# First token tile of an encoder layer loaded in two column halves, its squares split half, quarter, quarter, and one preset moved

## The chip, the cores and the metric

One core of one Trainium2 chip. The metric is device time of one execution in microseconds (us); three runs of the kernel before are given. Everything on the core is written out by hand: five engines (TensorE = PE, VectorE = DVE, ScalarE = ACT, GpSimd = POOL, SyncE = SP) each run their own list of instructions in order and wait for each other by semaphores.

## The reference

One layer of an encoder over 512 tokens of width 1024, in float32. The part that matters here is its head:

```python
u = rmsnorm(h, g_pre_mix[i])        # y = x * rsqrt(mean(x*x) + 1e-6) * g
proj = u @ w_in[i]                  # 1024 x 3840
qa, ka, va, qb, kb, vb, qc, kc, vc = jnp.split(proj, SPLIT_POINTS, axis=-1)
```

Behind it come three kinds of attention, gates, an output product with a norm and a residual, and a feed-forward part with a convolution of width 3, again with norms and a residual.

## The kernel before

The 512 tokens are four tiles of 128 (`x_tok[:, t, :]`, t = 0 to 3, token on the partition). Matrix products are made from float32 values split in a high and a low part: `high*high + high*low + low*high`, three matmuls each. So each operand needs a rounded copy (ACT, `w_hi`, `u_high`) and a difference (POOL `w_lo` for weights, DVE `u_low` for tokens).

The head of the program, tile by tile:

- SP issues the loads of tiles 0 and 1 (`load_x`, L636), then the first two weight tiles (L670, L654, L655), tiles 2 and 3, two more weight tiles, and the small tables (`load_small`, L642 to L650). Weight tiles go into a ring of four places.
- ACT squares and sums tiles 1 and 3 whole and tile 0's first 512 columns (`square`, L1046), into `norm_ss`. DVE sums the squares of tile 0's other 512 columns (L1605), already divided by 1024 and with the epsilon added, into `norm_ms`, and of tile 2 whole (L1622).
- POOL's `rstd` makes the mean (L882) and the power -0.5 (L885). For tile 0 it waits for both sums, by `squares` and `first_square`. Between these it makes the low quarters of the first weight tiles (`w_lo_quarter`, L899; later ones in `w_lo`, L871): its order is mean and power of tiles 0 and 1, four quarters of weight tile 0, one of weight tile 1, mean and power of tile 2, three quarters, mean and power of tile 3.
- DVE scales each tile by its power and the gain (tile 0 in two halves, L1611; the others L1591). The gain has been spread over the partitions by two matmuls (L2356).
- PE transposes the scaled tiles (L2362 for tile 0, L2342 for the others) and multiplies with the first two weight tiles (`value_products`, L2508) in an order written out by hand: tile 0 high by high, transposes of tile 1, tile 0 the rest, tile 1, transposes of tile 2, and so on. A few transposes of the identity (`keep_clock_up`, L2350) fill its time before.
- Before tile 0 is there, DVE presets four pieces of memory (L1600 to L1603). The last of them, `pages[0:CHUNK, Q_LO_PG:Q_LO_PG + 2, :]`, 64 x 1024 zeros, is needed by the first score product (`pe.wait_ge(q_lo_cleared, 2)` ahead of `qk(0)`).

## Time and profile before

| | |
|---|---|
| median of 3 runs | 841.32 us (840.88, 841.32, 843.56) |
| profiled execution, its own time | 841.03 us |
| its span, first to last instruction | 839.2 us |
| TensorE busy | 831.0 us (99%) |
| VectorE, ScalarE, GpSimd busy | 647.0, 478.9, 398.6 us |
| granted TensorE clock, mean | 0.999 |

The profile is of one execution. Its page gives busy time by engine, the chain of work that ended last, and groups of instructions; the trace can be asked for the timeline of a stretch, the waits, and the traffic. Times in rows are us from the start of the span, so they compare with 839.2, and the 1.8 us between span and time stand outside.

### The profile page before, as it was taken

To read this page: it belongs to the slowest core of one execution; us is meant where nothing else is said; L and a number is where in the kernel's file an instruction comes from. 1 tells how busy PE (TensorE), PEld (TensorE's weight loads), DVE (VectorE), ACT (ScalarE), POOL (GpSimd) and SP (SyncE) were. 2 spreads that over 40 slices of the span, in tenths; PEclk is the share of its full clock that TensorE was granted. 3 is DMA by queue.
4 is the path that set the end of the run, shared out by engine and by line. 5 is a ranking of instruction groups with operands and counts; after the bars stand their busy time and mean duration, and the time that the engine had idled before them with its cause. 6 is when DMAs were issued, how large, how long until landed. Compare 5 with 4: busy or idle time off the path is not lost.

```text
span 839.2 us, 13423 instructions
## 1 busy us (share of the span) xinstructions
PE 831.0 (99%) x4701; PEld 727.0 (87%) x4701; DVE 647.0 (77%) x1263; ACT 478.9 (57%) x905; POOL 398.6 (47%) x511
## 2 busy tenths in 40 slices
PE   8999999999999999999999999999999999999997
PEld 7888888888888888999998899899999999988885
DVE  6577777788776867966544389988888888999995
ACT  5475656777776664544443447556565656545662
POOL 6454434433352346986677426766565656010002
PEclk9999999999999999999999999999999999999999
DMA  7632133232223212334336631555554443396584
GB/s 238 175 102 73 53 100 100 75 99 57 82 80 69 80 44 82 114 114 120 95 101 218 201 134 52 187 174 170 170 171 118 121 119 121 132 312 242 170 285 157
DMA packets 138071, 111.35 MB, mean 133 GB/s; under 512 B 7607, under 2 KB 121215, under 8 KB 136724
## 3 DMA queue, kind: packets, MB, share of 16 engines
q1 hardware_dynamic: 136378, 102.05, 40.0%
q0 software_dynamic: 720, 5.24, 1.8%
q10 hardware_dynamic: 906, 3.20, 1.1%
q8 instruction: 38, 0.62, 0.3%
q14 instruction: 29, 0.24, 0.1%
HBM read 97.05 MB, written 13.42 MB: 132 GB/s over the span
## 4 chain that ended last, share of the span: by engine, by line
PE 97%; DVE 1%; DMA 0%; ACT 0%; issue 0%; POOL 0%; DVEq 0%; POOLq 0%
PE banks L2324 24%; PE banks L2326 24%; PE banks L2325 24%; PE banks L2626 3%; PE banks L2625 3%; PE banks L2624 3%; PE banks L2498 2%; PE banks L2407 2%; PE banks L2406 2%; PE banks L2794 1%; PE banks L2793 1%; PE banks L2795 1%; PE banks L2508 1%; PE banks L2470 1%; PE banks L2477 1%; PE banks L2342 1%
## 5 line engine op out<-in xcount | busy, mean ns | idle before, releaser
L871 POOL TENSOR_TENSOR ring_lo<-ring_raw,ring_hi 128x256 fp32r<-128x256 f32 x376 | 305.5, 846 | 278.1 <-ACT ring_hi L1036 277.8
L2324 PE MATMUL banks<-u_hi,ring_hi 128*128 128x512 f32 (+1 forms) x580 | 222.0, 383 | 0.0
L2326 PE MATMUL banks<-u_hi,ring_lo 128*128 128x512 f32 (+1 forms) x580 | 217.4, 375 | 0.0
L2325 PE MATMUL banks<-u_lo,ring_hi 128*128 128x512 f32 (+1 forms) x580 | 217.1, 374 | 0.0
L2326 PEld LDWEIGHTS banks<-u_hi,ring_lo 128*128 128x128 f32 x580 | 109.2, 188 | 20.0
L2325 PEld LDWEIGHTS banks<-u_lo,ring_hi 128*128 128x128 f32 x580 | 109.5, 189 | 18.1
L2324 PEld LDWEIGHTS banks<-u_hi,ring_hi 128*128 128x128 f32 x580 | 109.3, 188 | 17.8
L1036 ACT CAST ring_hi<-ring_raw 128x1024 fp32r<-128x1024 f32 x95 | 99.0, 1043 | 38.7 <-PE banks L2326 22.9
L2145 DVE SCALAR_TENSOR_TENSOR wide<-banks,cols,wide 128x511 f32<-128x511 f32 x88 | 64.6, 744 | 3.5 <-ACT wide L1402 1.6
L2324 PE MATMUL banks<-pages,ring_hi 128*128 128x512 f32 (+1 forms) x180 | 61.2, 340 | 0.0
L2325 PE MATMUL banks<-pages,ring_hi 128*128 128x512 f32 (+1 forms) x180 | 61.2, 340 | 0.0
L2326 PE MATMUL banks<-pages,ring_lo 128*128 128x512 f32 (+1 forms) x180 | 61.1, 340 | 0.0
L1191 ACT ACTIVATE scratch<-scratch,negmax 128x193 f32<-128x193 f32 (+5 forms) x96 | 49.4, 517 | 8.4 <-DVE negmax L1796 7.6
L882 POOL TENSOR_SCALAR norm_ms<-norm_ss 128x1 f32<-128x1 f32 x14 | 4.4, 311 | 95.2 <-ACT pages L1046 94.9
L1796 DVE CUSTOM_DVE_ANT_0 scratch<-banks,scratch 128x128 f32<-128x128 f32 (+3 forms) x64 | 28.9, 488 | 24.4 <-PE banks L2498 23.2
L2324 PE MATMUL banks<-ring_hi,pages 128*128 128x512 f32 x112 | 44.0, 393 | 0.0
L2326 PE MATMUL banks<-ring_hi,pages 128*128 128x512 f32 x112 | 43.6, 389 | 0.0
L2325 PE MATMUL banks<-ring_lo,pages 128*128 128x512 f32 x112 | 43.6, 389 | 0.0
L962 POOL TENSOR_TENSOR ring_lo<-ring_raw,ring_hi 128x256 fp32r<-128x256 f32 x44 | 37.6, 874 | 11.7 <-ACT ring_hi L1430 11.7
L1402 ACT ACTIVATE wide<-banks,cols 128x512 f32<-128x512 f32 x40 | 31.1, 776 | 21.1 <-DVE banks L2119 13.4
L2326 PEld LDWEIGHTS banks<-pages,ring_lo 128*128 128x128 f32 x180 | 34.2, 190 | 3.8
L2324 PEld LDWEIGHTS banks<-pages,ring_hi 128*128 128x128 f32 x180 | 34.2, 190 | 3.5
(339 smaller groups left out, 2004.7 us busy)
## 6 DMA issues: line engine op xcount, KB each, us to landing
ring_raw<-in_w_ffn_up_dram SPq DMA_DIRECT2D x88, 256.0 KB, 3.5
ring_raw<-in_w_in_dram SPq DMA_DIRECT2D x59, 256.0 KB, 3.4
ring_raw<-in_w_ffn_down_dram SPq DMA_DIRECT2D x55, 256.0 KB, 3.7
ring_raw<-in_w_gate_dram SPq DMA_DIRECT2D x48, 256.0 KB, 3.3
split_tokens<-pages SPq DMA_DIRECT2D x5, 1024.0 KB, 7.0
pages<-split_tokens POOLq DMA_DIRECT2D x5, 1024.0 KB, 6.6
ring_raw<-in_w_out_dram SPq DMA_DIRECT2D x16, 256.0 KB, 3.1
second_tokens<-wide SPq DMA_DIRECT2D x10, 384.0 KB, 3.9
```

Source lines behind the costliest of these rows:

```text
L871: last = pool.tensor_tensor(wlo[:, r, c], raw[:, r, c], whi[:, r, c].bitcast(F32), ALU.subtract)
L962: last = pool.tensor_tensor(dst[:, c], src[:, c], hi[:, c].bitcast(F32), ALU.subtract)
L1036: act.copy(whi[:, r, :], raw[:, r, :]).then_inc(w_hi_done, 1)
L1191: act.activation(p_out, p_in, ACT.Exp, scale=-1.0, bias=negmax[:, s % 2, m:m + 1], accum_out=rowsum[:, s % 2, m:m + 1]).then_inc(exp_done, 1)
L1402: act.activation(wide[:, 4 + 2 * j + c, :], psum[:, 2 * j + c, :], ACT.Identity, scale=cols[:, 88 + fc:89 + fc], bias=cols[:, 132 + fc:133 ...
L1796: dve.tensor_tensor_reduce(scratch[:, P_PAGE + m, c0:c0 + n], psum[:, SC_BANK + m, 0:n], scratch[:, BIAS_PAGE + b % 4, j0:j0 + n], -1.0, c ...
L2145: dve.scalar_tensor_tensor(out=y[:, back:SEQ], in0=psum[:, 2 * j + c, 0:SEQ - back], scalar=tap, in1=y[:, back:SEQ], op0=ALU.mult, op1=ALU ...
L2324: pe.matmul(out, lhs_hi, rhs_hi, start=start, stop=False)
L2325: pe.matmul(out, lhs_hi, rhs_lo, start=False, stop=False)
L2326: return pe.matmul(out, lhs_lo, rhs_hi, start=False, stop=stop)
L2624: pe.matmul(dst, w_h, u_h, start=False, stop=False, skip_group_check=True)
L2625: pe.matmul(dst, w_h, u_l, start=False, stop=False, skip_group_check=True)
```

## The change

Tile 0 is loaded by two DMAs, columns 0 to 511 with a semaphore of its own, `x_first`, and columns 512 to 1023 with `x_loaded[0]`. DVE sums the squares of the first half as soon as that is there, and then those of columns 768 to 1023, starting from the first sum; ACT squares columns 512 to 767 only. POOL waits for two counts of `first_square`. The second preset of q moves from ahead of the sums to between the scaling of tiles 2 and 3. The small loads use one semaphore fewer among them.

```diff
-        small_loaded = [sem(f"small_loaded{i}") for i in range(5)]
+        small_loaded = [sem(f"small_loaded{i}") for i in range(4)]
+        x_first = sem("x_first")
...
-            load_x(0)
+            sp.dma_start(x_tok[:, 0, 0:512], x_rows[0][:, 0:512]).then_inc(x_first, 16)
+            sp.dma_start(x_tok[:, 0, 512:1024], x_rows[0][:, 512:1024]).then_inc(x_loaded[0], 16)
             load_x(1)
...
-                    sp.dma_start(lam_in[:, i, :], v[0].partition_broadcast(P)).then_inc(small_loaded[4], 16)
-                sp.dma_start(sink[:], sinks[0].partition_broadcast(P)).then_inc(small_loaded[1], 16)
+                    sp.dma_start(lam_in[:, i, :], v[0].partition_broadcast(P)).then_inc(small_loaded[1], 16)
+                sp.dma_start(sink[:], sinks[0].partition_broadcast(P)).then_inc(small_loaded[0], 16)
...
-                    pool.wait_ge(first_square, 1)
+                    pool.wait_ge(first_square, 2)
...
-            square(0, 0, x_tok[:, 0, 0:512], 512)
+            square(0, 0, x_tok[:, 0, 512:768], 256)
...
-            dve.memset(pages[0:CHUNK, Q_LO_PG:Q_LO_PG + 2, :].bitcast(F32), 0.0).then_inc(q_lo_cleared, 1)
+            dve.wait_ge(x_first, 16)
+            dve.tensor_tensor_reduce(tmp[:, 0:512], x_tok[:, 0, 0:512], x_tok[:, 0, 0:512], 1.0 / D, EPS,
+                                     ALU.mult, ALU.add, norm_ms[:, 0, 3:4]).then_inc(first_square, 1)
             dve.wait_ge(x_loaded[0], 16)
-            dve.tensor_tensor_reduce(tmp[:, 0:512], x_tok[:, 0, 512:1024], x_tok[:, 0, 512:1024], 1.0 / D, EPS,
-                                     ALU.mult, ALU.add, norm_ms[:, 0, 0:1]).then_inc(first_square, 1)
+            dve.wait_ge(first_square, 1)
+            dve.tensor_tensor_reduce(tmp[:, 512:768], x_tok[:, 0, 768:1024], x_tok[:, 0, 768:1024], 1.0 / D,
+                                     norm_ms[:, 0, 3:4], ALU.mult, ALU.add, norm_ms[:, 0, 0:1]).then_inc(first_square, 1)
...
-            dve.wait_ge(first_square, 1)
+            dve.wait_ge(first_square, 2)
...
-            for t in (2, 3):
-                xs(0, t, x_tok[:, t, :], spread_gain())
+            xs(0, 2, x_tok[:, 2, :], spread_gain())
+            dve.memset(pages[0:CHUNK, Q_LO_PG:Q_LO_PG + 2, :].bitcast(F32), 0.0).then_inc(q_lo_cleared, 1)
+            xs(0, 3, x_tok[:, 3, :], spread_gain())
...
-                dve.wait_ge(small_loaded[4], 64)
+                dve.wait_ge(small_loaded[1], 64)
...
-                dve.wait_ge(small_loaded[0], 16)
+                dve.wait_ge(small_loaded[0], 2 * 16)
...
-                dve.wait_ge(small_loaded[1], 16)
```

The head of VectorE's list before (`ISA` is the sum of squares, with the read of its accumulator behind it):

```order
L1603 MEMSET pages 64x1024
L1605 ISA wide,norm_ms<-scratch 128x512 [waits x_loaded0]
L1605 ISA norm_ms 128x1
L1611 SCALAR_TENSOR_TENSOR scratch<-scratch,norm_rstd,banks 128x512 [waits gain_spread,rstd_done]
...
L1597 TENSOR_TENSOR u_lo<-banks,u_hi 128x8x128 [waits u_hi_done]
L1591 SCALAR_TENSOR_TENSOR scratch<-scratch,norm_rstd,banks 128x1024 [waits rstd_done] x2
```

and now, with the line numbers of the changed program:

```order
L1606 ISA wide,norm_ms<-scratch 128x512 [waits x_first]
L1606 ISA norm_ms 128x1
L1610 ISA wide,norm_ms<-scratch,norm_ms 128x256 [waits first_square,x_loaded0]
L1610 ISA norm_ms 128x1
L1616 SCALAR_TENSOR_TENSOR scratch<-scratch,norm_rstd,banks 128x512 [waits gain_spread,rstd_done]
...
L1599 TENSOR_TENSOR u_lo<-banks,u_hi 128x8x128 [waits u_hi_done]
L1593 SCALAR_TENSOR_TENSOR scratch<-scratch,norm_rstd,banks 128x1024 [waits rstd_done]
L1631 MEMSET pages 64x1024
L1593 SCALAR_TENSOR_TENSOR scratch<-scratch,norm_rstd,banks 128x1024 [waits rstd_done]
```

One sum of squares has become two, of which the second waits for the first, and the preset has moved behind the scaling of tile 2.

The head of SyncE's list before:

```order
L636 DMA scratch<-in_x_dram 128x1024 x2
L670 DMA ring_raw<-in_w_in_dram 128x2x256
```

and now:

```order
L639 DMA scratch<-in_x_dram 128x512
L640 DMA scratch<-in_x_dram 128x512
L637 DMA scratch<-in_x_dram 128x1024
L672 DMA ring_raw<-in_w_in_dram 128x2x256
```

Tile 0 takes two places in the queue, and everything behind it stands one place later.

## Rows read from the trace of the kernel before

**Rows 1.** The page, part 4: chain that ended last, by engine.
```profile
PE 97%; DVE 1%; DMA 0%; ACT 0%; issue 0%; POOL 0%; DVEq 0%; POOLq 0%
```
**Rows 2.** Waits of PE, whole span (us in total, times, longest us).
```profile
PE banks L2362 <- DVE scratch L1611: 0.5, 1, 0.5
PE banks L2508 <- ACT u_hi L1050: 0.2, 1, 0.2
```
**Rows 3.** Chain of waits in order of time, start (start us, us, what).
```profile
0.74 4.03 DMA scratch<-in_x_dram
...
5.72 0.28 POOL norm_ms L882
...
6.07 0.56 POOL norm_rstd L885
...
6.66 0.76 DVE scratch L1611
7.42 0.04 issue
...
8.88 0.94 PE banks L2508 x4
```
**Rows 4.** Timeline, first 15 us (start us, us, engine, instructions, [idle before]).
```profile
0.74 0.87 SPq L636 DMA_DIRECT2D scratch<-in_x_dram  x2
...
3.53 0.91 DVE L1603 MEMSET pages<- 64x1024 f32 x1 [0.27 <-issue]
...
4.79 0.63 ACT L1046 ACTIVATE pages<-scratch 128x512 fp32r<-128x512 f32 x1 [2.20 <-DMA scratch<-in_x_dram]
4.80 0.69 DVE L1605 CUSTOM_DVE_ANT_0 wide<-scratch 128x512 f32<-128x512 f32 x1 [0.36 <-DMA scratch<-in_x_dram]
...
6.08 1.06 ACT L1046 ACTIVATE pages<-scratch 128x1024 fp32r<-128x1024 f32 x1 [0.57 <-DMA scratch<-in_x_dram]
...
7.60 0.55 POOL L885 TENSOR_TENSOR norm_rstd<-norm_ms,minus_half 128x1 f32<-128x1 f32 x1
...
8.19 1.28 DVE L1591 SCALAR_TENSOR_TENSOR scratch<-scratch,norm_rstd,banks 128x1024 f32<-128x1024 f32 x1
...
9.66 1.03 PE L2342 MATMUL banks<-ident,scratch 128*128 128x128 f32 x8
...
13.58 1.28 DVE L1591 SCALAR_TENSOR_TENSOR scratch<-scratch,norm_rstd,banks 128x1024 f32<-128x1024 f32 x1 [0.40 <-POOL norm_rstd L885]
...
14.91 1.09 PE L2342 MATMUL banks<-ident,scratch 128*128 128x128 f32 x8
```
**Rows 5.** Traffic by stretch (last number GB/s); tile 2's issue and landing.
```profile
3.75:4.00 0.25, 0.25 (x3) 0.25 (x2) 0.25 (x1) 0.00 (x0) 0.00 (x0) 1.00 0.97 393
...
7.00:7.50 0.50, 0.04 (x1) 0.04 (x1) 0.50 (x2) 0.50 (x3) 0.17 (x1) 1.00 0.92 318
...
4.82 0.94 SPq L636 DMA_DIRECT2D scratch<-in_x_dram  x2
...
scratch<-in_x_dram SPq DMA_DIRECT2D x1, 512.0 KB, 5.8
```
**Rows 6.** Timeline of POOL's weight quarters and of VectorE, 8 to 17 us.
```profile
8.13 1.43 POOL L899 TENSOR_TENSOR ring_lo<-ring_raw,ring_hi 128x256 fp32r<-128x256 f32 x2
...
10.91 1.73 POOL L899 TENSOR_TENSOR ring_lo<-ring_raw,ring_hi 128x256 fp32r<-128x256 f32 x1
...
10.66 1.37 DVE L1622 CUSTOM_DVE_ANT_0 wide<-scratch 128x1024 f32<-128x1024 f32 x1
...
11.96 1.21 DVE L1597 TENSOR_TENSOR u_lo<-banks,u_hi 128x1024 fp32r<-128x1024 f32 x1
...
13.41 1.12 PE L2508 MATMUL banks<-ring_hi,u_lo 128*128 128x256 f32 x8
...
16.59 1.28 DVE L1591 SCALAR_TENSOR_TENSOR scratch<-scratch,norm_rstd,banks 128x1024 f32<-128x1024 f32 x1 [1.73 <-POOL norm_rstd L885]
```
**Rows 7.** Stretch of PE's first products (granted clock third from the end).
```profile
8.50:9.00 0.50, 0.39 (x4) 0.18 (x3) 0.50 (x1) 0.50 (x2) 0.50 (x2) 1.00 0.83 315
```

## The prediction

> **What bounds the kernel now.** I read the page first, then the waits of TensorE, then the chain of waits at the start, then the timeline of the first 20 us. The page's chain lies for 97% on TensorE [rows 1]. After its first instruction TensorE waits only twice in the whole execution: 0.5 us for the scaled token tile 0 and 0.2 us for the high part of tile 2 [rows 2]. So this is a kernel in which a delay or a gain before 20 us reaches the end one to one, and nothing later gives it back; and the change touches only what happens before 17 us. The question is what the start waits for.
>
> The chain at the start [rows 3] goes: landing of token tile 0 (0.74 + 4.03 = 4.77), ScalarE's squares, POOL's mean at 5.72 and power at 6.07, VectorE's scaling at 6.66, TensorE's transposes, first products at 8.88. The reader should see that this chain is drawn by the last releaser alone, and that a second chain runs beside it: tile 1. ScalarE idles 0.57 us and starts tile 1's squares at 6.08, on the landing; POOL's power for tile 1 ends at 7.60 + 0.55 = 8.15; VectorE, free about 0.1 us before, scales tile 1 from 8.19 to 9.47; TensorE transposes it from 9.66 [rows 4]. From POOL's 8.15 on hang also the low weight quarters, after them the mean of tile 2, its scaling 13.58 to 14.86, and its transposes on TensorE at 14.91 [rows 4]. VectorE's end at 7.42 (6.66 + 0.76) is taken up by TensorE at 7.46, so 0.04 us suffice between the two engines [rows 3]. Tile 1's chain is therefore only 0.19 - 0.04 = 0.15 us behind at 9.66 and 0.05 - 0.04 = 0.01 us behind at 14.91. **Tile 0 is not the only thing that the start waits for.**
>
> **The change, part by part.**
> 1. The load of tile 0 in two halves. SyncE issues two DMAs of 512 KB in 0.87 us [rows 4], so one more costs 0.43 us of its queue. The first half lands earlier than 4.77: 262 kB at the 393 GB/s that flowed from 3.75 to 4.00 [rows 5] are 0.67 us, so at about 4.10. The second half ends with the same last byte, at 4.77. Tile 1's issue moves from about 1.18 to 1.6, but its bytes flow only after tile 0's (tile 0 lands at 4.77, tile 1 at 6.08, 1.3 us for 524 kB, which is the full rate), so the later issue is covered by the backlog; if it were not, it would cost its 0.43. The same holds for tile 2, issued at 4.82 and landed 5.8 us later [rows 5]. Rows of 2 KB in place of 4 KB: the nearest rows are 393 GB/s where 4 KB rows flow and 318 GB/s in a stretch with 1 KB rows of weights [rows 5]; if all of tile 0 went at the lower rate it would take 1.65 instead of 1.33 us, +0.3. I take +0.03, as 2 KB is nearer to the large rows and most of the low rate is in mixed traffic. Bounds of this part for tile 1: 0 and +0.43.
> 2. Squares. ScalarE's 512 columns took 0.63 and 1024 took 1.06 [rows 4], so 256 take 0.63 - 0.21 = 0.42: 0.21 less. VectorE's 512 columns took 0.69 [rows 4]; 256 take 0.35 to 0.42. The first half's sum starts at 4.10 and ends with its accumulator read near 4.9, about 0.1 after the second half is there, because the second instruction waits for the first. It ends at about 5.3, ScalarE's at about 5.3 too. So POOL's mean starts at about 5.55 instead of 5.72: **-0.17** on tile 0's chain. Bounds: -0.21 if the first half lands by 3.95, and +0.4 if it lands no sooner than the whole (0.69 and then another 0.35 to 0.42, in a row).
> 3. The second preset of q leaves the place before the sums. Its 0.91 us from 3.53 to 4.44 [rows 4] were free, since the tile landed at 4.77; left there it would have held up the new first sum by 0.3. Now it stands between the scaling of tiles 2 and 3, where VectorE idled 1.73 us before 16.59 waiting for POOL [rows 6]: 14.86 + 0.91 = 15.77, done 0.8 before that. Cost 0 for VectorE; its reader, the first score product, is at the 39th microsecond. What is behind that cover is POOL: in that gap it does the last low quarter of weight tile 1 and the mean and power of tile 3. Nearest row for VectorE holding up POOL: a quarter takes 0.7 (two in 1.43), but the one from 10.91 took 1.73, beside the sum over tile 2 on VectorE from 10.66 to 12.04 [rows 6]. If the preset did the same, tile 3's scaling at 16.59 would slip by up to 0.91. So 0 to +0.91; I take 0, because the nearest row's instruction reads two operands from SBUF and a preset reads none.
>    The Trainium skill says the same in "SBUF — State Buffer", section on which engines share a port: a VectorE instruction with two SBUF inputs contends with a reading GpSimd instruction, one with at most one input outside the two-port modes does not. By that page the 1.73 us quarter is the lock, on which the trace agrees, and the sum has 0 for the preset; by the 1.73 us row alone it would be +0.9.
> 4. Semaphores of the small loads merged. The readers at 23 and 27 us come well after those landings; the extra SyncE issue may shift them by 0.43. Cost 0.
>
> **Sum.** Tile 0's chain gains 0.17. At 9.66 TensorE can use 0.15 of it, at 14.91 only 0.01 to 0.05, since tile 2's transposes hang on tile 1's landing by way of POOL. Tile 1 pays 0.03. Net: -0.05 + 0.03, or about -0.02. From the profiled execution's own 841.03 that is 841.0; the median of the three runs lies 0.29 above it, so **841.3** on that scale. What a measurement of this kernel can tell from no change is 0.3%, 2.5 us; I forecast that nothing can be told.
>
> **The rivals.**
> *The whole gain of tile 0 arrives.* For it: the chain of waits names tile 0 alone. Against it: the 0.01 us of room at 14.91. It would need tile 1 to land earlier too. Then -0.17 to -0.67 (the full head start of the first half): 840.6 to 841.1. Chance 0.12.
> *The lock changes its order.* VectorE's sum over tile 2 started at 10.66, inside POOL's fourth quarter, and got the port when that ended at 10.91 [rows 6]. Tile 2 is issued at 4.82 and lands 5.8 us later, at 10.62: only 0.04 before VectorE asks. If it lands more than 0.25 us later (one more DMA issue is 0.43), POOL's fifth quarter goes first, the sum starts at 11.6 and the low part of tile 1 behind it, which ended at 11.96 + 1.21 = 13.17, ends 0.7 to 0.8 late; TensorE took it up at 13.41 [rows 6] and so had about 0.2 us of room: +0.5, or 841.8. With the upper bound for tile 1's own landing added, +0.9, 842.2. Speaking against it is the backlog. Chance 0.11, slower but under 2.5 us. The Trainium skill, "DMA: Bandwidth & Descriptors", rules for kernel authors, speaks against splitting: many small transfers should be coalesced into one, and two transfers to disjoint partition halves serialize, since both use all 16 engines; column halves as here do so too. By that the first half buys little and tile 1 pays; the sum would be this rival's. No row here shows a split load.
> *The preset holds up POOL*, as in part 3: +0.9, 842.2. Chance 0.06.
> *TensorE runs slower for a stretch.* This one alone could be told from no change. The four products from 8.88 took 0.94 us, some 0.22 each from start to start [rows 3], while eight of the same shape took 1.12 from 13.41, 0.12 each [rows 6]; the granted clock reads 1.00, the 2.4 GHz level, in the stretch around 8.88 [rows 7], so the record doesn't settle what slows them. With the change TensorE has products done at about 9.4 and idles up to 0.2 us before 9.66, where it was busy. If the slow pace lasted on from there, each product would cost 0.1 more; some 25 of them make the 2.5 us, that is if the slow pace held until about 13 us. Against it: the idle before 7.46 gets shorter, not longer. 843.8 or more, chance 0.03.
>
> **How the numbers follow.** The forecast has 0.68, the rivals 0.12, 0.11, 0.06 and 0.03. Only the last leaves the 0.3%. From the forecast's share I give 0.01 to slower and 0.02 to faster by over 2.5, for what I haven't seen and for the scatter: one of three runs stood at 843.56, 2.2 above the median. Faster 0.02, within 0.94, slower 0.04. Range: the lowest run, 840.88, less the 0.17 and a little, is 840.6, with the tail of the first rival 840.5; upward the second and third rivals end at 842.2. So 840.5 to 842.2, leaving out the scatter and the clock.
>
> **What would show it.** Right: the first sum on VectorE starts about 4.1, POOL's first mean at 5.55, first transposes of tile 0 at about 7.3; ScalarE's squares of tile 1 still start near 6.08, tile 1's transposes near 9.6, tile 2's within 0.1 of 14.9; the quarter of 1.7 us is still there; VectorE's preset near 14.9 with quarters of 0.7 beside it; span 839.1 to 839.3. Wrong: squares of tile 1 before 5.9 or after 6.3; a POOL quarter beside the preset over 1 us; tile 2's transposes moved by over 0.2 either way; slow products past 9.7; or a TensorE wait after 20 us that wasn't there.

## The result and the profile after

| | before | changed | |
|---|---|---|---|
| median of 14 runs each, same chip | 840.93 us | 842.38 us | ratio 1.0018, 95% interval 1.001 to 1.0026 |
| lowest run | 840.37 | 841.25 | +0.88 |
| profiled execution | 841.03 | 842.04 | +1.01 |
| its span | 839.2 | 840.2 | +1.0 |

The change costs about 1 us in a single execution and 1.45 us between the medians (1.8 parts in a thousand, 0.8 to 2.2 us by the interval). That is within the 0.3% called "no change", but it isn't zero. The median lies above the range, which ended at 842.2; the profiled execution, 842.04, lies inside it. The runs scatter upward: 6 of the changed kernel's 14 took 843.8 us or more, where 2 of the 14 before took 843.6, so the shift of the medians is less sure than the 1.0 us of the two traces.

The page's chain is as before, 97% TensorE:

```profile
PE 97%; DVE 1%; DMA 1%; ACT 0%; issue 0%; DVEq 0%; SPq 0%; POOL 0%
```

The waits of TensorE over the whole span of the changed kernel (us in total, times, longest us), beside [rows 2]:

```profile
PE banks L2513 <- ACT u_hi L1063: 1.2, 1, 1.2
PE banks L2347 <- DVE scratch L1593: 0.2, 1, 0.2
PE banks L2513 <- ACT u_hi L1052: 0.2, 1, 0.2
```

The wait of 0.5 us for the scaled tile 0 [rows 2] is gone. There are two new ones: 0.2 for the scaled tile 1 (VectorE, L1593), and 1.2 ahead of tile 0's own first products, which stand before tile 1's transposes. They need ScalarE's rounded copy of tile 0 (`u_hi`, L1063). TensorE was ready for them early, since tile 0 came early. But ScalarE works through its list in order, and there the squares of tile 1 stand ahead of that copy. So tile 1's late landing holds up tile 0 as well: its first products start at 9.43, 0.55 later than before (8.88 [rows 3]), though its mean came earlier. This adds nothing to the loss, as TensorE then waits 0.2 for tile 1 all the same. The chain of waits at the start leads back to tile 1 (start us, us, what):

```profile
0.74 0.40 SPq L639
...
1.19 0.42 SPq L640
...
1.66 5.45 DMA scratch<-in_x_dram
...
7.14 1.16 ACT pages L1048 x2
...
8.38 0.20 POOL norm_ms L884
...
8.66 0.56 POOL norm_rstd L887
...
9.24 1.29 DVE scratch L1593
...
10.58 1.09 PE banks L2347 x8
```

In [rows 3] this chain began with tile 0's landing at 4.77. Now it begins with three issues on SyncE's queue, and the long piece is the landing of tile 1, issued at 1.66 and there at 7.11. The timeline of the first 27 us shows both tiles (start us, us, engine, instruction, [idle before <- releaser]):

```profile
1.66 0.52 SPq L637 DMA_DIRECT2D scratch<-in_x_dram  x1
...
3.62 0.69 DVE L1606 CUSTOM_DVE_ANT_0 wide<-scratch 128x512 f32<-128x512 f32 x1 [0.35 <-DMA scratch<-in_x_dram]
...
4.21 0.42 ACT L1048 ACTIVATE pages<-scratch 128x256 fp32r<-128x256 f32 x1 [1.62 <-DMA scratch<-in_x_dram]
...
4.47 0.49 DVE L1610 CUSTOM_DVE_ANT_0 wide<-scratch,norm_ms 128x256 f32<-128x256 f32 x1 [0.15 <-DVE norm_ms L1606]
...
5.18 0.26 POOL L884 TENSOR_SCALAR norm_ms<-norm_ss,norm_ms 128x1 f32<-128x1 f32 x1 [3.71 <-DVE norm_ms L1610]
...
7.14 1.06 ACT L1048 ACTIVATE pages<-scratch 128x1024 fp32r<-128x1024 f32 x1 [2.42 <-DMA scratch<-in_x_dram]
...
8.71 0.58 ACT L1063 CAST u_hi<-banks 128x512 fp32r<-128x512 f32 x1
...
9.43 0.93 PE L2513 MATMUL banks<-ring_hi,u_hi 128*128 128x256 f32 x4 [1.19 <-ACT u_hi L1063]
...
15.95 1.09 PE L2347 MATMUL banks<-ident,scratch 128*128 128x128 f32 x8
...
26.20 0.40 PE L2329 MATMUL banks<-u_hi,ring_hi 128*128 128x512 f32 x1
```

The reader should see three things. The first half was there by 3.6 and the second by 4.2, where the whole tile had landed at 4.77; POOL's mean came 0.54 earlier (5.18 against 5.72 [rows 3]). Tile 1's squares start 1.06 later (7.14 against 6.08 [rows 4]). And from there the delay is handed on undiminished: tile 1's transposes 10.58 against 9.66, tile 2's 15.95 against 14.91 [rows 4], and the first product of full width 26.20 against 25.17 in the kernel before.

The traffic of the changed kernel in five stretches of one microsecond (last number GB/s, ahead of it the busy share of the DMA engines):

```profile
1.50:2.50 1.00, 0.97 (x5) 0.97 (x6) 0.73 (x3) 1.00 (x1) 0.00 (x0) 1.00 0.53 170
2.50:3.50 1.00, 1.00 (x6) 1.00 (x5) 0.76 (x1) 0.09 (x1) 0.00 (x0) 1.00 0.96 344
3.50:4.50 1.00, 1.00 (x5) 0.77 (x4) 0.73 (x3) 0.29 (x1) 0.00 (x0) 1.00 0.82 289
4.50:5.50 1.00, 1.00 (x2) 0.34 (x1) 0.46 (x2) 0.22 (x2) 0.26 (x1) 1.00 0.85 284
5.50:6.50 1.00, 1.00 (x4) 0.36 (x3) 0.38 (x1) 0.00 (x0) 0.56 (x1) 1.00 0.67 206
```

and the same stretches of the kernel before:

```profile
1.50:2.50 1.00, 0.97 (x5) 0.97 (x6) 0.73 (x3) 1.00 (x1) 0.00 (x0) 1.00 0.62 115
2.50:3.50 1.00, 1.00 (x6) 1.00 (x5) 0.76 (x1) 0.09 (x1) 0.00 (x0) 1.00 0.92 258
3.50:4.50 1.00, 1.00 (x4) 0.77 (x4) 0.91 (x1) 0.00 (x0) 0.00 (x0) 1.00 1.02 401
4.50:5.50 1.00, 1.00 (x2) 0.34 (x1) 0.70 (x2) 0.71 (x2) 0.00 (x0) 1.00 0.98 375
5.50:6.50 1.00, 1.00 (x4) 0.44 (x3) 0.00 (x0) 0.43 (x2) 0.70 (x2) 1.00 1.08 377
```

A rate in GB/s over one microsecond is a number of kB, so the sums are what had moved by 6.5: 170 + 344 + 289 + 284 + 206 = 1293 kB after, 1526 before. The changed kernel is ahead until 3.5 us (514 against 373) and then moves 374 kB less in the next three microseconds, at 206 to 289 GB/s. The engines were busy for 0.82, 0.85 and 0.67 of these, against 1.02, 0.98 and 1.08 before. They weren't short of work: by 4.63 SyncE had issued tiles 0 and 1 and two weight tiles, 2.1 MB. A stretch between 3.5 and 6.5 us in which the busy share is under 0.9 is called a hole below.

Which rows moved can be read from the sizes of the packets. From 4.5 us on a row of tile 1 is a packet of 4 KB (in the kernel before the first few may still be tile 0's), a row of weights one of 1 KB, and those under 512 B carry no rows of either. The changed kernel, 4.5 to 5.5 and 5.5 to 6.5:

```profile
DMA packets 186, 0.28 MB, mean 284 GB/s; under 512 B 14, under 2 KB 151, under 8 KB 186
DMA packets 147, 0.21 MB, mean 206 GB/s; under 512 B 15, under 2 KB 124, under 8 KB 147
```

and the kernel before, in the same two stretches:

```profile
DMA packets 177, 0.37 MB, mean 375 GB/s; under 512 B 15, under 2 KB 109, under 8 KB 177
DMA packets 403, 0.38 MB, mean 377 GB/s; under 512 B 35, under 2 KB 403, under 8 KB 403
```

Before, 94 rows of weights and 68 of tokens start in the first stretch, and none of tile 1's in the second: tile 1 is through, and then come the weights. In the changed kernel 137 rows of weights and 35 of tile 1 start in the first, 109 and 23 in the second. So tile 1's last rows trail behind while weights that were issued after it already move, and the engines stand idle for a third of the second stretch. This view doesn't tell the 16 engines apart, so it doesn't say which of them trail.

The preset, at its new place, on VectorE:

```profile
16.05 0.91 DVE L1631 MEMSET pages<- 64x1024 f32 x1 [0.15 <-issue]
```

and POOL's low quarter of a weight tile beside it:

```profile
15.95 0.72 POOL L901 TENSOR_TENSOR ring_lo<-ring_raw,ring_hi 128x256 fp32r<-128x256 f32 x1
```

The quarter takes half of what two took in [rows 6], 1.43 / 2. The preset doesn't hold it up.

### The profile page after: what moved, and what is told of

It reads as the page before. It is cut to its first block, busy times and chain, and to the rows that moved or that the text cites. A ratio compares the mean times of both kernels' runs of the same rounds, so it can differ in the third digit from the quotient of the medians.

```text
span 840.2 us, 13427 instructions
## 1 busy us (share of the span) xinstructions
PE 831.3 (99%) x4701; PEld 727.0 (87%) x4701; DVE 648.9 (77%) x1265; ACT 478.4 (57%) x905; POOL 398.4 (47%) x511
## 4 chain that ended last, share of the span: by engine, by line
PE 97%; DVE 1%; DMA 1%; ACT 0%; issue 0%; DVEq 0%; SPq 0%; POOL 0%
PE banks L2329 24%; PE banks L2331 24%; PE banks L2330 24%; PE banks L2631 3%; PE banks L2629 3%; PE banks L2630 3%; PE banks L2503 2%; PE banks L2412 2%; PE banks L2411 2%; PE banks L2800 1%; PE banks L2798 1%; PE banks L2799 1%; PE banks L2513 1%; PE banks L2475 1%; PE banks L2482 1%; PE banks L2347 1%
```

## The experiments

All runs are set against the kernel before on the same chip in the same job. One table serves them all. "Tile 1" is the start of ScalarE's squares of tile 1; where ScalarE was still busy with tile 0, the landing was no later, which the table marks with ≤. "Full product" is the start of TensorE's first product of width 512 (25.17 before). "Rest" is the span less that start. kB is what had moved by 6.5 us. The ratio is worked out from the single runs and isn't the quotient of the two medians.

| kernel | place of tile 1's load | tile 1 | full product | span | rest | kB | median / before | ratio, 95% interval |
|---|---|---|---|---|---|---|---|---|
| before | SyncE, 2nd | 6.08 | 25.17 | 839.2 | 814.0 | 1526 | | |
| changed | SyncE, 3rd | 7.14 | 26.20 | 840.2 | 814.0 | 1293 | 842.38 / 840.93 | 1.0018, 1.001 to 1.0026 |
| e1 | SyncE, 2nd | 5.85 | 25.82 | 839.8 | 814.0 | 1560 | 841.58 / 841.17 | 1.0004, 0.9994 to 1.0014 |
| e2 | SyncE, 3rd | 7.55 | 26.60 | 840.6 | 814.0 | 1287 | 842.84 / 841.17 | 1.0015, 1.0 to 1.0029 |
| e3 | SyncE, 2nd | 5.86 | 25.30 | 839.4 | 814.1 | 1555 | 841.28 / 841.17 | 0.9997, 0.9985 to 1.0009 |
| e4 | SyncE, 2nd | 5.89 | 25.33 | 839.4 | 814.1 | 1607 | 841.67 / 841.17 | 1.0003, 0.9991 to 1.0015 |
| e5 | SyncE, 3rd | 6.38 | 25.84 | 839.8 | 814.0 | 1421 | 842.3 / 841.28 | 1.0014, 1.0002 to 1.0026 |
| e6 | ScalarE | ≤5.86 | 25.42 | 839.5 | 814.1 | 1591 | 841.35 / 841.28 | 1.0007, 0.9996 to 1.0019 |
| e7 | SyncE, 3rd and 4th | 6.88 | 25.95 | 840.0 | 814.1 | 1309 | 841.94 / 841.28 | 1.0007, 0.9997 to 1.0016 |
| e8 | SyncE, 3rd | 8.29 | 27.35 | 842.6 | 815.3 | 922 | 844.54 / 841.28 | 1.0036, 1.0022 to 1.0051 |
| e9 | SyncE, 2nd, issued later | 5.63 | 25.85 | 843.0 | 817.2 | 1476 | 842.0 / 841.12 | 1.0009, 0.9997 to 1.0021 |
| e10 | SyncE, 2nd | ≤6.40 | 25.93 | 839.9 | 814.0 | 1484 | 842.38 / 841.12 | 1.0017, 1.0005 to 1.0029 |
| e11 | SyncE, 5th | 6.88 | 25.92 | 839.9 | 814.0 | 1278 | 842.34 / 841.12 | 1.0015, 1.0005 to 1.0024 |
| e12 | SyncE, 3rd | 7.23 | 26.29 | 840.2 | 813.9 | 1266 | 842.0 / 841.12 | 1.0004, 0.9994 to 1.0013 |
| e13 | SyncE, 3rd | 7.55 | 26.62 | 840.7 | 814.1 | 1431 | 844.12 / 841.18 | 1.0045, 1.0026 to 1.0063 |
| e14 | ScalarE | 6.64 | 25.70 | 839.8 | 814.1 | 1602 | 841.87 / 841.18 | 1.0011, 1.0001 to 1.0021 |
| e15 | SyncE, 2nd | 5.96 | 25.02 | 839.1 | 814.1 | 1609 | 841.16 / 841.18 | 1.0004, 0.9994 to 1.0013 |

Read the column "rest" first. In 15 of 17 executions it is 813.9 to 814.1, whatever the start did; the full products start anywhere between 25.02 and 26.62. So **the span is 814.0 plus the start of the full product**, and an experiment on the start can be read from its trace to 0.1 us where the medians scatter by several tenths. The two exceptions, e8 and e9, have late waits of their own. The waits of TensorE in e9:

```profile
PE banks L2794 <- ACT banks L1570: 1.2, 1, 1.2
PE banks L2325 <- DVE u_lo L2215: 0.9, 1, 0.9
PE banks L2509 <- DVE u_lo L1598: 0.5, 1, 0.5
```

The first two end at 768 and 793 us; e8 has one of 0.9 us, ending at 793. In the other 15 profiled executions they don't occur, and [rows 2] don't show them.

### Which part of the change costs: e1, e2, e3, e12

**e1_whole_load**: the changed kernel, tile 0 loaded by one DMA.

```diff
-        x_first = sem("x_first")
...
-            sp.dma_start(x_tok[:, 0, 0:512], x_rows[0][:, 0:512]).then_inc(x_first, 16)
-            sp.dma_start(x_tok[:, 0, 512:1024], x_rows[0][:, 512:1024]).then_inc(x_loaded[0], 16)
+            load_x(0)
...
-            dve.wait_ge(x_first, 16)
+            dve.wait_ge(x_loaded[0], 16)
```

> Changed kernel with tile 0 loaded whole again; the squares stay split half, quarter, quarter. If the split load is the cause: squares of tile 1 at about 6.1 us; tile 0's mean on POOL starts later than before the change, about 6.1 instead of 5.72, since the sums over 512 and 256 columns run in a row after 4.77; tile 1's transposes at 9.7 to 10.0; time 0 to 0.4 us above before. If the squares or the preset are the cause, it stays 1 to 1.5 us above.

Tile 1 is back at 5.85. But without the half load VectorE's two sums stand in a row, POOL's mean comes at 6.15 instead of 5.72, and the full product at 25.82. The time, 0.4 us over before, is that of the squares' split without its early half, no longer that of tile 1.

**e2_split_load_only**: the kernel before, tile 0 by two DMAs, all else as it was.

```diff
-            load_x(0)
+            for h in range(2):
+                c = slice(512 * h, 512 * (h + 1))
+                sp.dma_start(x_tok[:, 0, c], x_rows[0][:, c]).then_inc(x_loaded[0], 16)
             load_x(1)
...
-            act.wait_ge(x_loaded[0], 16)
+            act.wait_ge(x_loaded[0], 32)
```

(The same wait on VectorE.)

> Kernel before with tile 0 loaded by two DMAs from SyncE, all else as before (both readers wait for both halves). If the split load itself makes tile 1 late: ScalarE's squares of tile 1 start near 7.1 us instead of 6.08, tile 1's transposes near 10.6 instead of 9.66, and the time is 1 to 1.5 us above the kernel before. If the split load is harmless and the new order of squares or the preset is to blame: squares of tile 1 at 6.1, time within 0.3 us of before.

The timeline of ScalarE in e2:

```profile
7.55 1.06 ACT L1048 ACTIVATE pages<-scratch 128x1024 fp32r<-128x1024 f32 x1 [2.48 <-DMA scratch<-in_x_dram]
```

This one edit brings tile 1's late landing, the wait for ScalarE's copy of tile 0 (here 1.5 us), and a full product at 26.60. It is the whole loss, and more.

**e3_preset_only**: the kernel before, with only the preset moved.

```diff
-            dve.memset(pages[0:CHUNK, Q_LO_PG:Q_LO_PG + 2, :].bitcast(F32), 0.0).then_inc(q_lo_cleared, 1)
...
-            for t in (2, 3):
-                xs(0, t, x_tok[:, t, :], spread_gain())
+            xs(0, 2, x_tok[:, 2, :], spread_gain())
+            dve.memset(pages[0:CHUNK, Q_LO_PG:Q_LO_PG + 2, :].bitcast(F32), 0.0).then_inc(q_lo_cleared, 1)
+            xs(0, 3, x_tok[:, 3, :], spread_gain())
```

> Kernel before with the second preset of q moved between the scaling of tiles 2 and 3. If the preset does not hold up POOL: the POOL quarter beside it takes 0.7 us, tile 3 is scaled from 16.6 us, time within 0.3 us of before. If it holds the port: a quarter of 1 us or more, tile 3 scaled up to 0.9 us later, time up to 0.9 us above.

No difference (ratio 0.9997). VectorE in e3 from 10.6 us on:

```profile
10.68 1.81 DVE L1621 CUSTOM_DVE_ANT_0 wide<-scratch 128x1024 f32<-128x1024 f32 x1 [0.24 <-DMA scratch<-in_x_dram]
...
14.98 0.91 DVE L1625 MEMSET pages<- 64x1024 f32 x1 [0.16 <-issue]
```

and POOL:

```profile
9.28 2.13 POOL L899 TENSOR_TENSOR ring_lo<-ring_raw,ring_hi 128x256 fp32r<-128x256 f32 x3
...
13.38 2.13 POOL L899 TENSOR_TENSOR ring_lo<-ring_raw,ring_hi 128x256 fp32r<-128x256 f32 x3
```

The three quarters from 13.38 take 0.71 each, and the preset at 14.98 lies across the third: again not held up. VectorE's line at 10.68 is the prediction's second rival, come by chance of the landing: tile 2 was a little late, VectorE's sum started 0.01 us after POOL's fifth quarter (10.67), and it took 1.81 us instead of 1.37 [rows 6]. The price was a wait of 0.3 us on TensorE (for the low part of tile 1), where 0.5 was said. The same order is in e1, e5 and e9, with waits of 0.2, 0.4 and 0.5 us.

**e12_changed_again**: the changed kernel once more, unedited.

> The changed kernel as it is, profiled a second time. If tile 1's late landing belongs to the change: squares of tile 1 again at 7 or later and 1 to 1.5 us above before. If it was an accident of one execution: squares near 6.1 to 6.5.

The trace repeats: tile 1 at 7.23, full product 26.29, span 840.2. The medians differ by less here (842.0 against 841.12) than in the first comparison (842.38 against 840.93). Where the trace says 1.0, two comparisons of medians said 1.45 and 0.9, and the interval of the second, 0.9994 to 1.0013, by itself doesn't exclude that nothing changed.

### Why tile 1 lands late: e4, e5, e6, e7, e9, e10, e11, e8

**e4_half_from_act**: the second half is issued on ScalarE's queue (at 0.75 us), so tile 1 is again second on SyncE's.

```diff
-            sp.dma_start(x_tok[:, 0, 512:1024], x_rows[0][:, 512:1024]).then_inc(x_loaded[0], 16)
...
+            act.dma_start(x_tok[:, 0, 512:1024], x_rows[0][:, 512:1024]).then_inc(x_loaded[0], 16)
             act.dma_start(g_row, g_pre_mix).then_inc(small_loaded[2], 16)
```

> Changed kernel with the second half of tile 0 issued on ScalarE's queue, ahead of the gain row, so that tile 1 has the second place in SyncE's queue again (issue near 1.2 us). If the later place in SyncE's queue is what makes tile 1 late: it lands near 6.1, squares of tile 1 at 6.1, time at or 0.1 to 0.3 us below before. If it is the two loads of 2 KB rows as such: squares of tile 1 stay near 7.1 and the time 1 to 1.5 us above before.

Tile 1 is there at 5.89. The rows are 2 KB as in the changed kernel, so rows of 2 KB alone don't delay it (though only one load of such rows is left ahead of it on its queue). But now the halves land together (the first sum on VectorE starts at 4.50), and POOL's mean comes at 6.07.

**e6_tile1_from_act**: the changed kernel, with tile 1 on ScalarE's queue behind the gain row.

```diff
-            load_x(1)
...
             act.dma_start(g_row, g_pre_mix).then_inc(small_loaded[2], 16)
+            act.dma_start(x_tok[:, 1, :], x_rows[1]).then_inc(x_loaded[1], 16)
```

> Changed kernel with tile 1 issued on ScalarE's queue behind the gain row, near 1.3 us, and both halves of tile 0 on SyncE's. If tile 1's late issue or its third place in SyncE's queue is the cause: squares of tile 1 at about 6.1, tile 0's mean on POOL still near 5.2, time 0 to 0.3 us below before. If not: squares of tile 1 above 7, time 1 us or more above before.

Traffic in e6:

```profile
1.50:2.50 1.00, 0.96 (x5) 0.97 (x6) 0.73 (x3) 0.81 (x1) 0.00 (x0) 1.00 0.58 131
2.50:3.50 1.00, 1.00 (x6) 1.00 (x5) 0.76 (x1) 0.47 (x1) 0.00 (x0) 1.00 0.94 326
3.50:4.50 1.00, 1.00 (x5) 0.78 (x4) 0.70 (x2) 0.00 (x0) 0.00 (x0) 1.00 1.01 387
4.50:5.50 1.00, 1.00 (x2) 0.34 (x1) 0.05 (x1) 0.05 (x1) 0.00 (x0) 1.00 0.98 367
5.50:6.50 1.00, 1.00 (x3) 0.34 (x1) 0.44 (x2) 1.00 (x3) 0.27 (x1) 1.00 1.09 380
```

The hole is gone, and tile 1 is there by 5.86. But it now shares the engines with tile 0's second half, which lands at 5.45; POOL's mean comes at 6.16, where 5.2 was expected. What tile 1 got back, tile 0 paid. The issue is only 0.36 us earlier than in the changed kernel (1.30 against 1.66), the landing at least 1.25. In the Trainium skill, "DMA: Bandwidth & Descriptors", section "Issuing engines are not separate DMA queues", a second issuing engine saves only the time of issue. Here that page and the measurement differ: on a second queue the load gained over three times what its issue gained. And with tile 0 whole the same move made it later (e14).

**e5_weights_held**: the changed kernel, SyncE waits for the first half before it issues weights (first weight DMA at 3.52).

```diff
+            sp.wait_ge(x_first, 16)
             for t, (kind, n) in enumerate(TILES):
```

> Changed kernel in which SyncE waits for the first half of tile 0 (landed at 3.6 us) before it issues the first weights. If weights issued from 2.2 us on slow tile 1's rows: tile 1 lands at 5.9 to 6.1, its squares start 1 us sooner than in the changed kernel, and the weights come later by up to 1.4 us. If tile 1 is late for its own place or rows: squares of tile 1 still at 7.1 or later.

Tile 1 at 6.38, between the two expectations: some 0.8 of the 1.06 is back, so in the changed kernel weights issued after tile 1 take engine time that tile 1 needs, as the packets above show too. Everything behind is issued later as well, tile 2 at 5.91 instead of 4.67. VectorE's sum of tile 2 starts only at 11.75, TensorE waits 0.4 us for the low part of tile 1, and the full product is at 25.84.

**e7_both_tiles_split**: tile 1 too is loaded in two column halves, third and fourth on the queue.

```diff
-            load_x(1)
+            for h in range(2):
+                c = slice(512 * h, 512 * (h + 1))
+                sp.dma_start(x_tok[:, 1, c], x_rows[1][:, c]).then_inc(x_loaded[1], 16)
```

(ScalarE's wait for tile 1 is for 32.)

> Changed kernel with tile 1 loaded in two column halves too, from SyncE's queue, the fourth place for its last half (issue near 2.1 us). If the mix of 2 KB rows followed by 4 KB rows is what makes tile 1 straggle: it lands by 6.2 in spite of the later issue, time within 0.3 us of before. If the place in the queue counts: it lands at 7.1 or later, as in the changed kernel or worse.

Tile 1 at 6.88, 0.26 better than the changed kernel and between the two expectations; the hole is there too, 199 GB/s from 3.5 to 4.5. Smaller pieces of tile 1 don't bring it back to 6.08.

**e9_tile1_issued_later**: the kernel before, SyncE waits for the identity (done at 1.48) before it issues tile 1. The load stays second, and is issued at 1.50, some 0.3 later.

```diff
             load_x(0)
+            sp.wait_ge(ident_done, 1)
             load_x(1)
```

> Kernel before, tile 0 whole, in which SyncE waits for POOL's identity (done at 1.48 us) before it issues tile 1, so tile 1 keeps the second place in the queue but is issued near 1.55 instead of 1.18 us. If the later time of the issue makes tile 1 late: its squares start at 7.0 or later, time 1 us or more above before. If it is the third place in the queue, or the split: squares of tile 1 within 0.2 of 6.1, time within 0.3 us of before.

Tile 1 lands earlier than ever on this queue, at 5.63. The time of the issue isn't what decides. The hole (258 and 272 GB/s) is now from 4.5 on. Tile 2 comes late: its sum on VectorE starts only at 11.24, TensorE waits 0.5 us for the low part of tile 1, and the full product is at 25.85, 0.7 late. So the expected time, within 0.3 us of before, was missed by the start; the profiled span, 843.0, carries the two late waits shown above besides.

This trace shows one thing more. Tile 0, whole and with the squares as before, is there by 4.25, and POOL's mean comes at 5.21; in e8, below, by 4.24 and also at 5.21. That is as early as in the changed kernel (4.21 and 5.18). In both, the next load of 512 KB is issued later than in the kernel before (1.50 and 1.67 against 1.19). So tile 0's gain in the changed kernel isn't shown to be the work of its halves: it can be that tile 1, issued later, took less from it.

**e10_second_half_third**: first half, tile 1, second half.

```diff
             sp.dma_start(x_tok[:, 0, 0:512], x_rows[0][:, 0:512]).then_inc(x_first, 16)
+            load_x(1)
             sp.dma_start(x_tok[:, 0, 512:1024], x_rows[0][:, 512:1024]).then_inc(x_loaded[0], 16)
-            load_x(1)
```

> Changed kernel with the order first half of tile 0, tile 1, second half of tile 0 on SyncE's queue. If what stands third on this queue straggles: tile 1 lands by 6.0 and the second half of tile 0 lands at 6 or later, with tile 0's mean on POOL after 6.5. If the split as such slows tile 1: it lands at 7 or later although issued near 1.2 us. Time 0.5 to 1.5 us above before in both cases.

Now the second half lands at 5.99, and tile 1 is in time. That is as expected for a third load that straggles, but it doesn't show one: the two tiles together are 1049 kB, and their last bytes land at 5.99 here and at 6.08 in the kernel before. There is no hole either (busy shares 1.01, 0.95 and 1.06 from 3.5 on). What was put last comes last, and no later than its bytes. POOL's mean is at 6.70, TensorE waits 1.3 us for tile 0, and the full product is at 25.93.

**e11_quarters**: tile 0 in four DMAs of 256 columns, tile 1 fifth, issued at 2.60.

```diff
-            sp.dma_start(x_tok[:, 0, 0:512], x_rows[0][:, 0:512]).then_inc(x_first, 16)
-            sp.dma_start(x_tok[:, 0, 512:1024], x_rows[0][:, 512:1024]).then_inc(x_loaded[0], 16)
+            for c0 in (0, 256):
+                sp.dma_start(x_tok[:, 0, c0:c0 + 256], x_rows[0][:, c0:c0 + 256]).then_inc(x_first, 16)
+            for c0 in (512, 768):
+                sp.dma_start(x_tok[:, 0, c0:c0 + 256], x_rows[0][:, c0:c0 + 256]).then_inc(x_loaded[0], 16)
```

(The waits for both semaphores are for 32.)

> Changed kernel with tile 0 in four DMAs of 256 columns (rows of 1 KB), tile 1 in the fifth place, issue near 2.6 us. If each DMA ahead of tile 1 costs it about as much as the first did (1.06 us for one more): tile 1 lands at 8 or later, the time is 2 us or more above before. If only the issue time counts, 0.47 us for each: landing near 7.5 to 8. If it was chance: as the changed kernel or earlier.

Tile 1 at 6.88: issued 0.94 later than in the changed kernel, landed 0.26 earlier. The delay doesn't grow with the place. The first two expectations fall; the third calls it chance, which e12 and e2 speak against. Here too the early part of tile 0 is early (3.69) and the late part late (5.56).

**e8_small_load_between**: the kernel before, with the 4 KB load of the sinks, 32 bytes a row to 128 partitions, between tiles 0 and 1.

```diff
             load_x(0)
+            sp.dma_start(sink[:], sinks[0].partition_broadcast(P)).then_inc(small_loaded[1], 16)
             load_x(1)
...
-                sp.dma_start(sink[:], sinks[0].partition_broadcast(P)).then_inc(small_loaded[1], 16)
```

> Kernel before, tile 0 whole, with the 4 KB load of the sinks moved from the end of the small loads to between tiles 0 and 1 on SyncE's queue. Tile 1 then has the third place, issue near 1.66 us, without any split. If the place alone makes tile 1 late: its squares start at 7.0 or later and the time is 1 us or more above before. If it needs the split rows: squares of tile 1 at 6.1 to 6.3, time 0 to 0.3 us above.

This was meant as "third place with almost no bytes". It is something else. Its traffic:

```profile
2.50:3.50 1.00, 1.00 (x6) 1.00 (x5) 0.76 (x1) 0.09 (x1) 0.00 (x0) 1.00 0.90 332
3.50:4.50 1.00, 1.00 (x5) 0.78 (x4) 0.97 (x2) 0.26 (x1) 0.00 (x0) 1.00 0.74 63
4.50:5.50 1.00, 1.00 (x2) 0.34 (x1) 0.49 (x2) 0.46 (x2) 0.27 (x1) 1.00 0.30 43
```

Two microseconds in which nearly nothing moves, tile 1 at 8.29, and 3.3 us on the median. So it says nothing on the place alone, and much on tiny rows in front of a large load.

### Is it the weights on the same queue: e13, e14, e15

**e13_first_weights_from_act**: the changed kernel, the first weight tile's three DMAs on ScalarE's queue (1.30 to 2.70).

```diff
             act.dma_start(g_row, g_pre_mix).then_inc(small_loaded[2], 16)
+            first_w, w_src = raw[:, 0, :].rearrange("p (k n) -> p k n", n=2 * P), win_v[:, 0:4, VA:VA + 2 * P]
+            act.dma_start(first_w[:, 0:2, :], w_src[:, 0:2, :]).then_inc(first_raw, 16)
+            for k in (2, 3):
+                act.dma_start(first_w[:, k, :], w_src[:, k, :]).then_inc(raw_loaded[0], 16)
```

(SyncE's own issues of that tile go. The second weight tile stays: SyncE issues it behind tile 1, from 2.13 on, so its queue doesn't hold the tokens alone, as the expectation has it.)

> The changed kernel, with the first weight tile's three DMAs issued on ScalarE's queue, so that SyncE's queue holds only the three activation loads (and the gain and identity rows) at the start. Theory A (the load in third place on SyncE's queue lands late because that one queue also carries the weights, and its engines run underfilled): tile 1's squares start by 6.2 us, no microsecond after 2.5 us is under about 320 GB/s, the first full product starts near 25.5 us and the time is 841.2 to 841.6. Theory B (third place alone makes it late, whatever shares the queue): tile 1's squares start at 7.0 to 7.3, the first full product near 26.2, the time 842.0 to 842.4.

Theory A falls, by 1.3 us, and Theory B's 7.0 to 7.3 is passed as well. Traffic in e13:

```profile
1.50:2.50 1.00, 0.97 (x5) 0.97 (x6) 0.73 (x3) 0.00 (x0) 0.00 (x0) 1.00 0.45 135
2.50:3.50 1.00, 1.00 (x6) 1.00 (x5) 0.76 (x1) 0.77 (x1) 0.00 (x0) 1.00 1.00 211
3.50:4.50 1.00, 1.00 (x5) 0.77 (x4) 0.33 (x1) 0.51 (x1) 0.00 (x0) 1.00 0.95 312
```

The first weight tile on another queue doesn't help. That no weights at all behind tile 1 would, isn't excluded. The engines are busy (shares 1.00 and 0.95 in the last two stretches shown), though at 211 and 312 GB/s where the kernel before has 258 and 401, and 1431 kB had moved by 6.5, more than in the changed kernel. Still tile 1 is later than in the changed kernel (7.55), and so is tile 0 (mean at 5.89), as the weights on the other queue now run beside it. Only 5 runs were taken of this kernel, 842.5 to 847.4; the trace gives +1.5 on the span.

**e14_before_tile1_from_act**: the kernel before, tile 1 on ScalarE's queue behind the gain row, as the edit of e6.

> The kernel before, first token tile whole, with tile 1's load issued on ScalarE's queue behind the gain row (near 1.3 us). Theory A (two queues keep the DMA engines filled): tile 1's squares start by 5.9 us, no stretch of a microsecond under 320 GB/s after 2.5 us, the first full product at 25.2 to 25.4, the time within 0.3 us of the kernel before. Theory B (which queue carries it is indifferent, only the bytes ahead count): the same time, but with a stretch under 300 GB/s somewhere before 6.5 us.

Neither holds. There is no hole (319 to 406 GB/s from 2.5 on), as Theory A had it, yet tile 1's squares start at 6.64, 0.56 later than on SyncE's queue, though the load is issued only 0.1 later. Full engines don't make a given tile early: which tile they carry counts. From 3.5 to 5.5 they carried 237 rows of weights beside 113 of tile 1, by the packets.

**e15_before_weights_from_act**: the kernel before with the first weight tile on ScalarE's queue, as the edit of e13.

> The kernel before, with the first weight tile's three DMAs issued on ScalarE's queue and tiles 0 and 1 alone on SyncE's. Theory A (two queues fill the engines): tile 1 lands near 5.6 to 6.0 and the time is within 0.3 us of the kernel before; an earlier weight tile can bring nothing, as the first products wait for the activations. Theory B (the weights on another queue take an equal share from tile 1): tile 1's squares start at 6.3 or later and the time is 0.3 to 0.8 us longer.

As Theory A said. The best of all traces: mean at 5.45, tile 1 at 5.96, the full product at 25.02. The span is 0.1 us under that of before, the median the same (841.16 against 841.18). None of the versions is measurably faster than the kernel before.

Put side by side, ten of the executions (before, e1, e3; changed, e12, e2; e15, e13, e14, e6) make a table of the start of tile 1's squares:

| what else is on ScalarE's queue | tile 0 whole | tile 0 in halves |
|---|---|---|
| nothing (all on SyncE's) | 6.08, 5.85, 5.86 | 7.14, 7.23, 7.55 |
| the first weight tile | 5.96 | 7.55 |
| tile 1 | 6.64 | ≤5.86 |

In the first two lines tile 1 stands behind tile 0 on one queue, and the halves cost it 1.1 to 1.7 us. In the third it doesn't, and they cost it nothing. The loss is that of the load **behind the two halves on their own queue**, whichever of the two queues carries the first weight tile.

## Why the prediction was wrong

*What bounds the kernel.* Right: a delay before 20 us reaches the end one to one. The table's rest of 814.0 shows it. Right too, and what mattered most: tile 0 isn't the only thing that the start waits for. By the prediction, tile 1's chain was 0.15 us behind at 9.66 and 0.01 behind at 14.91; so the 0.54 that tile 0's mean gained was worth at most that, and the 1.06 that tile 1 lost came through nearly whole (1.04 at tile 2's transposes, 1.03 at the full product, 1.0 in the span).

*Part 1, the load.* **Here is the step that failed**: "the later issue is covered by the backlog; if it were not, it would cost its 0.43", with +0.03 taken. Measured +1.06 (+1.15 in e12, +1.47 in e2): over twice the upper bound. The bound was made of the issue alone, as if a load that is issued 0.47 later could land at most 0.47 later. It assumed that the engines flow full, at 393 GB/s [rows 5], as long as anything is queued. They didn't: 284 and 206 GB/s with a megabyte queued. And it assumed that bytes leave in the order of issue ("its bytes flow only after tile 0's"). Already in the kernel before 774 kB had moved by 4.5 us (115 + 258 + 401), 250 more than tile 0 holds, and tile 0 was there only at 4.77. In the changed kernel 246 rows of weights started from 4.5 to 6.5 us beside 58 of tile 1, and e5, which holds the weights back, gives 0.8 back. The same assumptions mis-sized the halves, to the other side: "at about 4.10" and "at 4.77" came out as 3.6 and 4.2. Tile 2's issue, which was to be 0.43 later, came at 4.67, 0.15 earlier, since SyncE's first weight issue took 0.43 and not 1.14. Two of the prediction's own signs of being wrong are there: tile 1's squares after 6.3, and tile 2's transposes moved by over 0.2.

Rows of 2 KB as such were a fair worry; by themselves they aren't the cause (e4, e6).

*Part 2, the squares.* 256 columns took 0.42 on ScalarE, as said, and 0.49 on VectorE, where 0.35 to 0.42 was said. The mean came 0.54 earlier instead of 0.17, all of it from the landings. Whether the split brought that is open: in e8 and e9 the whole load and the old squares gave a mean at 5.21.

*Part 3, the preset.* Cost 0, as taken; the row of 0.72 us and e3 show it. The weighing of the 1.73 us row by what the instruction reads was right, and the Trainium skill's rule in "SBUF — State Buffer", section "Who interferes with whom" (two SBUF inputs on VectorE contend with a reading GpSimd instruction, at most one outside the two-port modes doesn't), agrees with both rows: the quarter beside the sum of two operands is slow, the one beside the preset isn't.

*Part 4, the semaphores.* No wait after 20 us was added. Cost 0.

*The sum* was -0.02; with +1.06 in the place of +0.03 it is +1.0, which is what the two traces show. What the sum didn't have is the way over ScalarE: tile 0's first products wait for a copy that stands behind tile 1's squares, so with tile 1 late nothing of tile 0's gain was left (9.43 against 8.88).

*The rivals.* The whole gain of tile 0 didn't arrive. The order of the lock did not flip in the changed kernel (a quarter of 1.73 is there again); it did in e1, e3, e5 and e9, at 0.2 to 0.5. TensorE wasn't slower: the four products at 9.43 took 0.93 us, as before (0.94), and the next four 0.72. The second rival's passage on the Trainium skill ("DMA: Bandwidth & Descriptors", rules for kernel authors: transfers should be coalesced) had the sign right, since tile 1 paid for the split; the page speaks of small transfers, though, under 64 KB above all, and these halves are of 256 KB. But the first half did not land only a little earlier, as the rival had it, but by over a microsecond. The upper price of that rival, 0.9, is near what came, by luck: it was made of the lock's 0.5, which didn't occur here, and the issue's 0.43.

*The range* ended at 842.2, for a median of 842.38. It had no case in which tile 1 is late by more than its issue. That the median fell outside is in part chance: ten more runs of the same kernel (e12) have a median of 842.0, inside the range. The step was wrong in both.

What stays open is why tile 1's last rows trail. A hole in the traffic goes with it often, but isn't the cause by itself. The engines' busy share falls under 0.9 somewhere between 3.5 and 6.5 us in all six kernels that have tile 1 behind all parts of tile 0 and the weights on the same queue (changed, e2, e5, e7, e11, e12), and in e8. But e9, with whole loads, has such a hole too, and there tile 1 was early; and e13 has none, and with e2 the latest tile 1 but e8's. "Third place on the queue" and "behind two half loads" aren't fully told apart for tile 1, as a third load behind two large whole ones was not tried; e10, whose third load lands when the same bytes land in the kernel before, and e11, where the fifth place costs less than the third, speak against the place.

## What to carry to other kernels

A load that is cut in two isn't only a load that arrives in two pieces: every load behind it on its queue moves back a place, and in this kernel the load behind the halves paid 1.1 to 1.7 us for it, not the 0.43 us of an issue. Bound such a price by a landing seen in a trace. Where one engine's list has the second tile's work ahead of the first's, as ScalarE's here, a late second tile holds up the first too. Before the first tile is made faster, look how far behind it the second tile's chain is; here there was 0.01 us of room, so that even a perfect split could bring next to nothing. And find the point from which the rest of the program takes a constant time (here the first full product, 814.0 before the end), as it reads a change of the start to 0.1 us.

## What the runs showed of the hardware

- A load of 32-byte rows to 128 partitions, 4 KB in all, ahead of a load of 512 KB on one queue: 63 and 43 GB/s for two microseconds, and the large load 2.2 us late (8.29 against 6.08). In the kernel before, the same load is issued at 15.91, and no wait of TensorE follows it [rows 2].
- Two queues share the engines, and a load that moves to the second one can take from the first: in e6 the second half of tile 0 was there at 5.45, in e13 at 5.17, where it was at 4.21 and 4.54 in the two executions of the changed kernel.
- On one queue, rows of a load can start after rows of loads issued behind it: in the changed kernel 23 rows of tile 1 (issued at 1.66) started from 5.5 to 6.5 us beside 109 rows of weights (issued from 2.22 on), after 137 such rows in the microsecond before.
- In the first 5 us issues on SyncE's queue take 0.38 to 0.57 us each, but single ones took over a microsecond: in the kernel before that of the first weights, 1.14; in e12 that of tile 1, 1.11, with nearly the same landing (squares from 7.23 against 7.14). After 6 us some took 1.6 us and more.
- Landings of the same load scatter by 0.1 to 0.3 us: in the two executions of the changed kernel tile 1 at 7.14 and 7.23, the second half of tile 0 at 4.21 and 4.54; in before and e3, which load alike, tile 1 at 6.08 and 5.86.
